# Expert gates summed in an HBM table by single-element indirect DMAs, expert inputs placed ahead of expert outputs

## What is computed

```python
def _peer(h, w_q, sub_keys, u_emb, v_emb):
    q = (tok @ w_q).astype(F32).reshape(n_tok, PEER_HEADS, 2, PEER_HALF)
    s = jnp.einsum('nhpc,hpkc->nhpk', q, sub_keys.astype(F32))
    s_top, i_top = lax.top_k(s, PEER_TOPK)
    ...
    best, pos = lax.top_k(cand, PEER_TOPK)
    expert = jnp.take_along_axis(cand_idx, pos, axis=-1)
    gate = jax.nn.softmax(best, axis=-1)
    ...
        act = jax.nn.gelu(jnp.einsum('tkd,td->tk', u_emb[eb], tb), approximate=False) * gb
        return jnp.einsum('tk,tkd->td', act, v_emb[eb])
```

## Time and profile before

| | us |
|---|---|
| median of 3 runs | 1700.28 |
| lowest and highest run | 1698.94, 1702.59 |
| span of the profiled execution | 1701.3 |
| TensorE busy in the span | 1646.9 |
| VectorE busy | 1174.0 |
| ScalarE busy | 801.9 |
| GpSimd busy | 99.0 |

### The profile page before, as it was taken

One profiled execution on the slowest core, in us unless ns is written; L12 is line 12 of the kernel. 1 busy time (PEld: TensorE's weight loads), 2 busy tenths in 40 slices (PEclk: granted clock), 3 DMA queues, 4 the chain that ended last, 5 costly groups with the idle time before them and its releaser, 6 DMA issues.

```text
span 1701.3 us, 32624 instructions
## 1 busy us (share of the span) xinstructions
PE 1646.9 (97%) x12606; PEld 1510.4 (89%) x12606; DVE 1174.0 (69%) x2143; ACT 801.9 (47%) x1223; POOL 99.0 (6%) x124
## 2 busy tenths in 40 slices
PE   8999999999999999989999989999999999999998
PEld 3999978999999998879898878999999999999997
DVE  3756656777846769647498998666666666666665
ACT  2423436566634675425213993444444444444444
POOL 0000000022200001110052000000000000000000
PEclk9999999999999999999999999999999999999999
DMA  8876414545554433204333015555555555455553
GB/s 307 303 272 223 149 50 149 189 175 191 179 176 149 152 144 125 101 4 158 115 124 124 26 50 187 185 195 176 196 178 192 185 185 193 177 197 176 194 183 126
DMA packets 38826, 278.94 MB, mean 164 GB/s; under 512 B 4432, under 2 KB 4560, under 8 KB 5328
## 3 DMA queue, kind: packets, MB, share of 16 engines
q1 hardware_dynamic: 35424, 254.82, 42.1%
q0 software_dynamic: 2304, 16.78, 2.6%
q10 hardware_dynamic: 1008, 6.05, 0.9%
HBM read 276.58 MB, written 1.05 MB: 163 GB/s over the span
## 4 chain that ended last, share of the span: by engine, by line
PE 86%; DVE 7%; ACT 4%; issue 2%; DMA 1%; DVEq 0%; POOL 0%; SPq 0%; ACTq 0%; POOLq 0%
PE ps L462 86%; DVE piece L1730 2%; DMA ring<-in_stream 1%; ACT piece L1217 1%; DVE pconst_sb L2483 1%; DVE cols L2483 0%; DMA arena<-in_xT 0%; DVE late L2483 0%; DVE arena L1780 0%; ACT arena L1256 0%; DVE arena L1833 0%; DVEq L2483 0%; ACT arena L1575 0%; ACT L1252 0%; DVE arena L1797 0%
## 5 line engine op out<-in xcount | busy, mean ns | idle before, releaser
L462 PEld LDWEIGHTS ps<-h_r,piece 128*128 128x128 f32 x5664 | 699.2, 192 | 19.8 <-issue 8.7
L462 PE MATMUL ps<-h_r,piece 128*128 128x256 f32 x5664 | 708.4, 284 | 4.6 <-DVE piece L1730 3.7
L1730 DVE TENSOR_TENSOR piece<-ring,piece 128x1024 fp32r<-128x1024 f32 x434 | 533.2, 1237 | 241.7 <-ACT piece L1217 240.3
L1217 ACT ACTIVATE piece<-ring 128x1024 fp32r<-128x1024 f32 x432 | 452.6, 1056 | 356.8 <-PE ps L462 352.7
L462 PE MATMUL ps<-piece,late_r 128*128 128x512 f32 x1536 | 370.1, 391 | 1.4 <-DVE late_r L2505 1.4
L462 PEld LDWEIGHTS ps<-piece,late_r 128*128 128x128 f32 x1536 | 281.1, 188 | 55.3 <-issue 1.8
L2500 DVE TENSOR_TENSOR late<-late,arena 128x256 f32<-128x256 f32 x113 | 72.0, 638 | 117.6 <-ACT late L1686 117.6
L1686 ACT ACTIVATE late<-ps 128x256 f32<-128x256 f32 x113 | 43.5, 385 | 200.5 <-PE ps L462 200.5
L462 PE MATMUL ps<-arena,ring 128*128 128x256 f32 x480 | 110.5, 379 | 1.6 <-DVE arena L1797 1.6
L462 PEld LDWEIGHTS ps<-arena,ring 128*128 128x128 f32 x480 | 88.1, 190 | 12.3 <-issue 2.0
L462 PE MATMUL ps<-arena 64*64 64x64 f32 (+7 forms) x930 | 87.4, 297 | 7.6 <-DVE arena L2266 1.8
(11 more groups left out here) (325 smaller groups left out, 1709.5 us busy)
## 6 DMA issues: line engine op xcount, KB each, us to landing
ring<-in_stream SPq DMA_DIRECT2D x240, 1024.0 KB, 4.8
arena<-in_mod POOLq DMA_DIRECT2D x16, 1024.0 KB, 6.2
arena<-in_const ACTq DMA_DIRECT2D x1, 2256.0 KB, 10.6
arena<-in_const ACTq DMA_DIRECT2D x1, 1648.0 KB, 8.8
xres<-in_xT SPq DMA_DIRECT2D x1, 1024.0 KB, 5.3
arena<-in_xT SPq DMA_DIRECT2D x1, 1024.0 KB, 7.1
arena<-in_subk ACTq DMA_DIRECT2D x1, 1024.0 KB, 4.9
out<-arena SPq DMA_DIRECT2D x4, 256.0 KB, 2.1
```

Source lines behind the costliest of these rows:

```text
L462: mm_last[0] = nc.tensor.matmul(*args, **kw)
L1217: A(piece[:, 0, c % 3], ring[:, p % RING, s], ACT.Copy).then_inc(S["hi_ready"], 1)
L1730: TT(piece[:, 1, c % 3], ring[:, p % RING, s], piece[:, 0, c % 3].bitcast(F32), ALU.subtract).then_inc(S["lo_ready"], 1)
```

## The change

- The gate table moves to HBM: `gate_table`, 4194304 elements of 4 bytes (16.8 MB), laid out expert group, expert, token. `G`, the one-hots, the transposes, `selT` and the gate stage on TensorE, VectorE and ScalarE go.
- GpSimd zeroes the table with 16 plain DMAs of 1 MB during the feed-forward stage of the first block (pages `up`).
- The softmax of the gates is done head by head on VectorE and ScalarE inside the selection (`gate_arg` to `gate_end`, `gate_exp`), and VectorE works out each address, (expert number) x 256 + token.
- GpSimd adds the gates into the table with 256 indirect DMAs, each of 128 single elements (one per partition) with an accumulate: 8 heads x 2 halves of the tokens x 16 places (`scatter`). For heads 1 to 7 the first DMA of a half waits until the 16 of the same half in the head before have landed.
- All 128 ups come first (16 unsplit and 112 split), and their gelus stay in the arena (`z_at`). Then come the 128 downs in a row.
- SP loads the gates of two groups at a time (`gate_in`, 256 KB in rows of 1 KB) into `gtile`, three deep. The first of these waits on SP for all scatters, and the pages for the third and later downs are behind it in SP's queue. `gate` multiplies in place, with both inputs contiguous.

The core of the diff:

```diff
-EARLY = 15
-CHOICE = 10
+CHUNK = 4
+EARLY = 16
...
+            pages_split(PAGE["ups"] + RING, NU // 2 - 2, 2 * (WHOLE0 - SPLIT0))
+            def gate_in(m, i=0):
+                sp.dma_start(gtile[:, m % RING], gate_pair[m + RING * i]).then_inc(g_in[m % RING], 16)
+            for tt in range(2):
+                sp.wait_ge(scat[tt], 2048)
+            gate_in(0)
+            lows = 2 * (WHOLE0 - SPLIT0) + NU
+            for m in range(1, 3):
+                sp.wait_ge(S["lo_ready"], lows + 2 * (m - RING) + 2)
+                page(PEER + m)
+                gate_in(m)
...
+            g.memset(zero, 0.0).then_inc(S["zero_set"], 1)
             with pool.Fori(0, 3) as i:
                 for u in range(LOOP):
                     gated_page(u, i)
+                    if u < 5:
+                        pool.dma_start(gate_zero[u + 5 * i], zero).then_inc(S["zeroed"], 16)
+            pool.dma_start(gate_zero[15], zero).then_inc(S["zeroed"], 16)
             for u in range(18, 22):
+                if u == 21:
+                    pool.wait_ge(S["zeroed"], 256)
                 gated_page(u)
...
+            def scatter(hh, first, last):
+                pool.wait_ge(S["gate_at"], 2 * hh + 2)
+                pool.wait_ge(S["gate_w"], hh + 1)
+                for n in range(first, last):
+                    tt, k = n // 16, n % 16
+                    if hh and k == 0:
+                        pool.wait_ge(scat[tt], 256 * hh)
+                    g.indirect_dma_start(gtab[:, :], bass.IndirectOffsetOnAxis(ap=gidx[:, hh, tt, k:k + 1], axis=0),
+                                         gw[:, hh, tt, k:k + 1], None, compute_op=ALU.add).then_inc(scat[tt], 16)
+            number(0)
+            for hh in range(1, 7):
                 number(hh)
+                scatter(0, CHUNK * (hh - 1), CHUNK * hh)
+            scatter(0, 6 * CHUNK, 32)
+            for hh in range(1, 8):
+                scatter(hh, 0, 32)
...
+            for n in range(4):
+                up(EARLY + n, C0 + n)
+            with pe.Fori(0, 9) as i:
+                for n in range(4, 4 + 2 * LOOP):
+                    up(EARLY + n, C0 + n, i)
+            with pe.Fori(0, 10) as i:
+                for e in range(2 * LOOP):
+                    down(e, C1 + e, i)
+            for e in range(20 * LOOP, P):
+                down(e, C1 + e)
...
+            for e in range(EARLY - 2):
+                gelu(e)
+                if e in (1, 4, 7, 11):
+                    gate_exp(4 + (1, 4, 7, 11).index(e))
...
+            def gate(e, i):
+                m, b = e // 2, e % 3
+                dve.wait_ge(g_in[m % RING], 16 * (m // RING + 1 + LOOP // RING * i))
+                dve.wait_ge(S["piece_used"], piece_no(PEER) + e - 1 + 2 * LOOP * i)
+                a_t = gtile[:, m % RING, e % 2, :]
+                TT(a_t, a_t, z_of(e, i), ALU.mult).then_inc(S["a_chain"], 1)
```

More of the change, by code:

```diff
@@ L46 @@
 WHOLE0 = PAGE["wq"]
-NWHOLE = PAGE["first"] - WHOLE0
+NWHOLE = PAGE["ups"] - WHOLE0
 def piece_no(p):
@@ L1107, in early_up @@
                 whole(PAGE["early"] + e // 2, e % 2, ps[:, T % 2, 0:L]).then_inc(S["acc_ready"], 1)
[L1109 removed]
+            for e in range(EARLY):
                 early_up(e)
[L1111 to L1117, removed]
@@ L1147, in _ @@
[L1147 to L1157, removed]
+            C0, C1, T0 = piece_of(PAGE["ups"]), piece_of(PAGE["peer"]), TURN["peer"]
@@ L1692, in _ @@
[L1692 to L1700 removed]
+            def gelu(e, i=0):
+                evac(TURN["peer"] + e, z_of(e, i), ACT.Gelu, slice(0, L), i, LOOP)
+            UPS, PEER = PAGE["ups"], PAGE["peer"]
@@ new lines, in _, with ups_page @@
+            for e in range(EARLY - 2):
+                gelu(e)
+                if e in (1, 4, 7, 11):
+                    gate_exp(4 + (1, 4, 7, 11).index(e))
+            split(UPS)
+            gelu(EARLY - 2)
+            gelu(EARLY - 1)
+            def ups_page(u, i=0):
+                split(UPS + 1 + u, i)
+                for s in range(2):
+                    gelu(EARLY + 2 * u + s, i)
+            for u in range(2):
+                ups_page(u)
+            with act.Fori(0, 3) as i:
+                for u in range(2, 2 + LOOP):
+                    ups_page(u, i)
@@ L1701, in _ @@
+            with act.Fori(0, 6) as i:
+                for u in range(20, 20 + LOOP):
+                    ups_page(u, i)
+            with act.Fori(0, 10) as i:
+                for u in range(1, 1 + LOOP):
+                    split(PEER + u, i)
+            for u in range(1 + 10 * LOOP, P // 2):
+                split(PEER + u)
             act.wait_ge(S["a_ready"], P)
@@ new lines, in _ @@
+            gate_end(7)
+            UPS, PEER = PAGE["ups"], PAGE["peer"]
+            for u in range(2):
+                split(UPS + u)
+            with dve.Fori(0, 9) as i:
+                for u in range(2, 2 + LOOP):
+                    split(UPS + u, i)
+            def gate(e, i):
[4 more added lines that the diff above has]
+                TT(a_t, a_t, z_of(e, i), ALU.mult).then_inc(S["a_chain"], 1)
+                dve.wait_ge(S["a_chain"], 2 * e + 1 + 4 * LOOP * i)
@@ L2525, in _, with down_page @@
-            for u in range(LOOP * rounds, P - EARLY):
-                split(PAGE["peer"] + 1 + u)
-                gate(EARLY + u, 0, gelu_t[:, (EARLY + u) % 2, :])
+            def down_page(u, i=0):
+                for s in range(2):
+                    low(PEER + u, s, i)
+                    gate(2 * u + s, i)
+            for u in range(10):
+                down_page(u)
+            with dve.Fori(0, 3) as i:
+                for u in range(10, 10 + LOOP):
+                    down_page(u, i)
@@ L2529, in _ @@
+            with dve.Fori(0, 6) as i:
+                for u in range(28, 28 + LOOP):
+                    down_page(u, i)
             dve.wait_ge(S["fg_in"], 16)
@@ L2575, in lay_out @@
         n += len(part)
-    blocks = list(u[:EARLY]) + list(v[:EARLY - 2])
-    for e in range(EARLY, P):
-        blocks += [v[e - 2], u[e]]
-    blocks += [v[P - 2], v[P - 1]]
+    blocks = list(u) + list(v)
     for k, block in enumerate(blocks):
```

279 lines of the change are left out of this document (83 added, 196 removed).

## The result

| | before | after |
|---|---|---|
| median, us (4 runs each, side by side) | 1700.47 | 1981.74 |
| lowest and highest run | 1698.94, 1702.59 | 1977.95, 1983.88 |
| ratio, 95% interval | | 1.1651 (1.1635 to 1.1668) |
| span of the profiled execution | 1701.3 | 1979.1 |

The prediction was 1622.8 us, faster. It was wrong by 359 us and in sign.

What follows compares the result with a forecast made beforehand. TensorE, busy 97% of the span, was taken as the bound. 77.3 us leaving it plus a 1.4 us wait, less 1.2 for two more unsplit ups, saved 77.5: span 1623.8, median 1622.8, range 1616 to 1712.

Steps and rivals of the forecast that it cites:

- What leaves TensorE: Gate-making between unsplit and split ups: 77.3 us of transposes, one-hot matmuls and waits go; net 77.5 us saved.
- Feeders in the downs: In the run of downs, VectorE needs 2.3 of 2.75 us each; DMA share 0.67 at 238 GB/s, covered by three buffers.
- Zeroing: Feed-forward stage: zeroing DMAs beside weight pages bring the DMA share to 0.95; cost taken as 0, range 0 to 5 us.
- Selection: Head selection among the unsplit ups: 8 us longer, last address by 934 against a 943.8 deadline, cost 0.
- The 20 others fit in the 4.3 us that GpSimd idles in each head: During selection: 20 of the 256 indirect DMAs hide in GpSimd's idle time, leaving 236 behind the last `number` at 917.
- The price of an indirect DMA: On GpSimd, c us for each indirect DMA, taken as 1.1; the stream of 236 ends at 1177, 83 us ahead of need.
- break-even of 1.78: GpSimd's stream of 236: at 1.78 us for each indirect DMA the 77.5 us gain is used up.
- The upper bound of 2.1 us: Price of an indirect DMA on GpSimd if each waited for the one before to land, as an HBM store does.
- nothing in the program waits for landing within a head: GpSimd's stream: landing is awaited only once in 16 DMAs, for DMAs issued at least 16 before, so the price is nearer the lower end.
- the queue becomes the bound: Rival, chance 0.19: GpSimd can't outrun landing; at 2.1 us each, 917 + 496 + 5 = 1418, span 1777, 76 us slower.
- threshold of 1.45: GpSimd's stream before the first down: nothing is late if 917 + 236 c + 5.3 <= 1265.2, c being us per DMA.
- The contention on SBUF: VectorE's two-operand remainders in the ups could hold GpSimd's address fetch, adding 0.26 us per DMA: 1.36 in place of 1.1.

Runs made afterwards that it cites:

- the run without the sum steps: Changed kernel with indirect DMAs that write plainly instead of adding, and 4096 bytes a partition for descriptors in place of 1024: 1621.84 us, span 1620.0.

## Why the prediction was wrong

- **What leaves TensorE: right.** With the stream out of the way the downs begin at 1265.78 (predicted 1265.2) and the span is 1620.0 (1623.8).
- **Feeders in the downs: right.** DMA share 0.67 and 239 GB/s, predicted 0.67 and 238. In the run of downs VectorE's cast begins 0.45 us behind the multiply (estimate 0.37) and the subtraction 0.33 behind the cast, and in each period of 2.72 us it idles 0.37:

```profile
1701.06 0.42 DVE L2473 TENSOR_TENSOR early<-early,arena 128x256 f32<-128x256 f32 x1
1701.51 0.29 DVE L2475 CAST late_r<-early 128x256 fp32r<-128x256 f32 x1
1701.84 0.42 DVE L2477 TENSOR_TENSOR late_r<-early,late_r 128x256 fp32r<-128x256 f32 x1
1702.64 1.23 DVE L1686 TENSOR_TENSOR piece<-ring,piece 128x1024 fp32r<-128x1024 f32 x1 [0.37 <-ACT piece L1211]
```

- **Zeroing: right.** From 339 to 470, where the zeroing lies in the kernel after, TensorE is busy 129.6 of 131 us at a DMA share of 0.85 (estimate 0.95).
- **Selection: wrong by 15.2 us.** The 16 unsplit ups took 70.5 us and not 55.3: 11.7 us of waits, the rest at the lower clock behind them. "The 20 others fit in the 4.3 us that GpSimd idles in each head" rested on c = 1.1. Four at 1.87 us or more don't. The last number ended at 944.1 and not at 917, which put the whole stream 27 us later. With short DMAs it ended at 918.2, as predicted.
- **The price of an indirect DMA: the step that failed.** I took c = 1.1 us, by doubling a plain DMA that moves long rows, and put waits inside the issue at nothing. Measured are 2.85 in the mean of the 236. Taken apart: 1.27 us are GpSimd's own for 128 single elements without a sum (0.97 and 0.30); the sum adds 0.6; VectorE's two-operand instructions add 0.1 to 0.2 beside the ups; the rest, 0.7 to 1.2 us, are waits that get shorter with more room for descriptors. At 1.87 the first two alone pass the break-even of 1.78. The upper bound of 2.1 us, "if each waited for the one before to land", was no bound: the mean was over it.
- **The argument "nothing in the program waits for landing within a head"** was true of the semaphores only. Room for descriptors is a wait that no semaphore shows, and the profile files it under "issue". It made the rival "the queue becomes the bound" true, with its mechanism nearly as written ("few can be in flight") and a larger price: by its formula 944.1 + 236 x 2.85 + 5.3 gives 1622.0, against 1622.27 measured. It had 0.19. The same formula, with each run's own last number and price, gives 1333.8, 1422.2 and 1473.1 for the runs without the sum, with 4096 bytes and with 2048; measured are 1333.23, 1422.56 and 1473.14. So price and deadline account for the whole wait.
- **The weighing of the bounds.** The two ends, 0.53 and 2.1, lay on both sides of a threshold of 1.45 and a break-even of 1.78. Nothing in the trace was near the operation, so most of the chance should not have stood on one side.
- **The contention on SBUF** was estimated in the prediction at 0.26 us, from the length and share of the remainders. SBUF — State Buffer of the Trainium skill (Who interferes with whom) says that "A DVE instruction with two SBUF inputs contends with a GpSimd instruction that reads SBUF". The trace agrees in kind: with room enough, a DMA takes 0.97 us alone and about 1.5 where it meets a remainder, 1.44 in place of 1.27 from start to start, so 0.17. DMA: Bandwidth & Descriptors of the Trainium skill (Anatomy of one DMA) says of making descriptors "You can emit a lot of descriptors before the incremental cost shows up". Here the descriptors did show up: 128 single elements cost 0.97 us against 0.53 for 128 rows, and 1.56 with the sum.

## What to carry to other kernels

A stream of small DMAs from one engine is a pipeline with a rate; before building on it, time one of its kind by itself, and compare its rate with the deadline. If the price is unknown and the deadline lies between the bounds, give both sides a real chance. When starts in such a stream have gaps that no semaphore explains, try more room for descriptors, which is one constant, and take the sum out of the transfer if an idle engine can make it. Here the room gave 200 us and then the plain writes 159; in the other order the plain writes gave 289 and then the room 70. The two edits overlap: both shorten the same gaps.

## What the runs showed of the hardware

- An indirect DMA of 128 single elements with a sum is 144 packets and 1.56 us of GpSimd, a plain one 32 packets and 0.97 us, where no two-operand instruction of VectorE meets it; 0.30 us lie between two at the least.
- Room for descriptors: 1024, 2048 and 4096 bytes in each partition give 2.56, 2.05 and 1.93 us for one DMA with a sum where nothing else is moved, 3.16, 2.36 and 2.11 beside the pages. Plain ones don't wait at all with 4096: in the run without the sum steps no gap is over 0.31 us. What frees the room was not taken apart; that pages make the waits longer speaks for the landing of earlier DMAs, but no run shows it.
- Idle time of TensorE also costs clock. In the 345 us it was granted half (1.2 GHz), and still half when the downs began (windows of 4 us, the columns as above, the clock third from the end):

```profile
1622.00:1626.00 4.00, 3.73 (x9) 2.96 (x10) 3.09 (x6) 1.06 (x1) 0.00 (x0) 0.50 1.04 420
1626.00:1630.00 4.00, 4.00 (x16) 3.20 (x15) 2.42 (x5) 1.06 (x1) 0.00 (x0) 0.78 0.99 390
1630.00:1634.00 4.00, 4.00 (x19) 3.33 (x18) 3.47 (x8) 1.52 (x2) 0.00 (x0) 1.00 0.65 214
```

The 1536 matmuls of the downs took 351.0 us here and 348.3 in the run that had no wait, so that was 2.7 us. In the other runs with a wait ahead of the downs, of 8.2 to 370.2 us, the downs took 1.5 to 3.0 us more, and the longer wait did not cost more: 2.9 at 8.2 us, 1.5 at 370.2.
